# A hybrid decoder step: the attention heads' norm inside the GLU stage, operands split in parts, router products moved, scratch memory shared

## The reference

```python
a = a * lax.rsqrt(jnp.mean(a * a, axis=-1, keepdims=True) + RMS_EPS) * lp['subln_g'] * (1.0 - lam_init)
out = g * jax.nn.sigmoid(g @ w_glu.astype(f32) + b_glu.astype(f32))
mix = jnp.concatenate([a, s], axis=-1) @ lp['w_out']
x = layer_norm(DN_ALPHA * x + mix, lp['ln1_g'], lp['ln1_b'])
```

## Time and profile before

| | us |
|---|---|
| median of 3 runs | 1306.68 (1303.94 to 1307.88) |
| the profiled execution's own time | 1303.61 |
| its span, first to last instruction | 1301.5 |
| head_norm starts (DVE) | 500.07 |
| first GLU product on PE | 518.48 |
| first projection matmul | 556.12 |
| first and last full router transposes | 581.11 and 697.48 |
| ACT's first instruction of `route` | 710.65 |

### The profile page before, as it was taken

How to read it: one execution, slowest core, us unless ns; L and a number is a source line. 1 busy time by engine, 2 the same in 40 slices (tenths; PEclk the granted TensorE clock), 3 DMA queues, 4 the chain that set the end, 5 groups by cost and what they waited for, 6 DMA issues and landing times. The chain is left out here.

```text
span 1301.5 us, 17352 instructions
## 1 busy us (share of the span) xinstructions
PE 1094.6 (84%) x5512; PEld 895.8 (69%) x5513; DVE 689.7 (53%) x1287; ACT 515.4 (40%) x752; POOL 325.7 (25%) x541
## 2 busy tenths in 40 slices
PE   7998999995998695989996258999999999999720
PEld 5886788993666584577774247888888888778510
DVE  3653735503888112445443835544447678675527
ACT  4232321424777312521111043544446567465313
POOL 0807184402000100000000011334233543445315
PEclk9998999996999866988897578999999999999965
DMA  6132221117600402632221074666778799987434
GB/s 223 41 105 53 91 53 50 33 23 278 192 1 1 151 1 72 216 152 97 97 89 54 0 290 157 228 207 206 236 237 309 252 310 411 351 274 245 109 127 164
DMA packets 51249, 201.33 MB, mean 155 GB/s; under 512 B 9107, under 2 KB 15635, under 8 KB 45043
## 3 DMA queue, kind: packets, MB, share of 16 engines
q1 hardware_dynamic: 40674, 138.43, 30.0%
q0 software_dynamic: 7488, 27.27, 8.6%
q10 hardware_dynamic: 3024, 34.87, 6.9%
HBM read 163.81 MB, written 36.73 MB: 154 GB/s over the span
## 5 line engine op out<-in xcount | busy, mean ns | idle before, releaser
L2014 DVE TENSOR_TENSOR wlo<-raw,whi 128x4096 fp32r<-128x4096 f32 x48 | 211.5, 4423 | 95.7 <-ACT whi L1943 95.6
L1943 ACT ACTIVATE whi<-raw 128x4096 fp32r<-128x4096 f32 x48 | 174.9, 3649 | 93.2 <-SPq L1816 38.7
L1852 POOL DMA_INDIRECT acc<-eyb,idxs x25 | 68.1, 2722 | 156.8 <-ACT eyb L1961 156.8
L1885 PE MATMUL psY<-whi,ehs 128*128 128x512 f32 x200 | 82.1, 411 | 9.7 <-DVE wlo L2014 9.7
L1885 PE MATMUL psG<-whi,exs 128*128 128x512 f32 x200 | 83.3, 416 | 4.5 <-DVE exs L2019 4.4
L1887 PE MATMUL psG<-whi,exs 128*128 128x512 f32 x200 | 80.8, 404 | 0.0
L1886 PE MATMUL psG<-wlo,exs 128*128 128x512 f32 x200 | 80.8, 404 | 0.0
L1886 PE MATMUL psY<-wlo,ehs 128*128 128x512 f32 x200 | 79.9, 400 | 0.0
L1887 PE MATMUL psY<-whi,ehs 128*128 128x512 f32 x200 | 79.8, 399 | 0.0
L1885 PE MATMUL psU<-whi,exs 128*128 128x512 f32 x200 | 79.3, 396 | 0.0
L1886 PE MATMUL psU<-wlo,exs 128*128 128x512 f32 x200 | 79.2, 396 | 0.0
(11 more groups left out here) (389 smaller groups left out, 2481.8 us busy)
## 6 DMA issues: line engine op xcount, KB each, us to landing
raw<-in_moe_w_gate SPq DMA_DIRECT2D x16, 2048.0 KB, 8.8
raw<-in_moe_w_up SPq DMA_DIRECT2D x16, 2048.0 KB, 16.7
raw<-in_moe_w_down ACTq DMA_DIRECT2D x16, 2048.0 KB
w_raw<-in_w_in SPq DMA_DIRECT2D x27, 256.0 KB, 3.2
stg<-in_x_prompt SPq DMA_DIRECT2D x8, 512.0 KB, 4.3
kc<-in_cache_k SPq DMA_DIRECT2D x16, 256.0 KB, 3.0
vc<-in_cache_v SPq DMA_DIRECT2D x16, 256.0 KB, 3.0
raw<-in_x_prompt SPq DMA_DIRECT2D x8, 512.0 KB, 6.4
```

The lines of the kernel that those rows point to most:

```text
L1852: nc.gpsimd.indirect_dma_start(s.acc, bass.IndirectOffsetOnAxis(ap=idxs[:, 0:1], axis=0), yb[j][:, :], None, compute_op=ALU.add).then_inc( ...
L1885: pe.matmul(out, hi, w_hi, start=(k == 0), stop=False)
L1943: nc.scalar.activation(whi[:, at], s.raw[:, at], ACT.Copy).then_inc(hi_made[i], 1)
L2014: nc.vector.tensor_tensor(wlo[:, at], s.raw[:, at], whi[:, at].bitcast(F32), ALU.subtract) \
```

## The change

- `head_norm` is removed as a stage; its work moves into `mix`. The scaling of block i + 1 stands on DVE behind the gate product of step i (`scale_o`), the transposes of block i on PE behind GLU product i (`turn_o`), into banks 4 and 5, and the copies on ACT behind tanh i (`keep_o`).
- `wg` is loaded at the end of SP's work in `sample`.
- `high_a` and `low_a` work on parts: part 0 is the four column blocks from `aT`, parts 1 to 4 one column block from `sT` each. For blocks 0 and 1 part 0 is made in step 4, parts 1 to 3 in steps 5, 8 and 11, part 4 at the end. PE waits for each part where it first uses it.
- The projection is issued in halves; the router products of block b - 1 stand between the halves of block b + 1, and `xT` has memory of its own. ACT copies the logits of block b - 1 after the square root and the roundings of block b.
- SP issues `gcol`, the bias, the `w_out` row blocks, and only then the x blocks, the router and LayerNorm weights, the padding rows; expert 0's gate weights wait until all of `o` is scaled, its up weights for the last transposes of `an`, the last GLU product and the padding stores.
- `raw` is allocated before attention and holds `o`, `v`, `wg`, `an`, the zero rows and part of attention's scratch; `kT` and `sT` share `s.ks`.

```diff
 # sample, SP
                 load_pages(sp, io, s, "cache_v", vc, m["v_in"])
+                sp.dma_start(s.wg, io["ssm_w_glu"][0].rearrange("(k p) n -> p k n", p=P)).then_inc(m["glu_in"], 16)
+                sp.wait_ge(m["glu_in"], 16)
 # mix, SP
-                sp.dma_start(wg[:, :, :], io["ssm_w_glu"][0].rearrange("(k p) n -> p k n", p=P)).then_inc(wg_in, 16)
+                sp.dma_start(gcol[:, :], io["subln_g"].rearrange("o v -> v o")).then_inc(g_in, 16)
...
+                sp.wait_ge(scaled, NBLK)
+                sp.dma_start(s.raw[:, slice(*PIECES[0])], expert_weights(io, 0, 0)).then_inc(first_in, 16)
+                sp.wait_ge(o_turned, NBLK)
+                sp.wait_ge(z_made, len(glu))
+                sp.wait_ge(pad_sent, 32)
+                sp.dma_start(s.raw[:, slice(*PIECES[1])], expert_weights(io, 0, 1)).then_inc(first_in, 16)
 # mix, PE
+                def turn_o(b):
+                    r = rows(b)
+                    pe.wait_ge(scaled, b + 1)
+                    if b >= 2:
+                        pe.wait_ge(o_kept, b - 1)
+                    for h in range(H):
+                        last = pe.transpose(bk[4 + b % 2][:, h * P:h * P + r], an[b % 2][0:r, h * P:(h + 1) * P],
+                                            s.ident[0:r, 0:r])
+                    last.then_inc(o_turned, 1)
                     last.then_inc(z_made, 1)
-                pe.wait_ge(s_made, len(glu))
+                    if i < NBLK:
+                        turn_o(i)
...
+                    for k in range(KD):
+                        if half == 0 and (k == 0 or k >= 4):
+                            pe.wait_ge(a_split, part_no(b, max(0, k - 3)) + 1)
...
-                project_out(0)
+                project_half(0, 0)
+                project_half(0, 1)
                 for b in range(NBLK):
                     if b + 1 < NBLK:
-                        project_out(b + 1)
-                    logits(b)
+                        project_half(b + 1, 0)
+                    if b >= 1:
+                        logits(b - 1)
+                    if b + 1 < NBLK:
+                        project_half(b + 1, 1)
+                    turn(b)
+                logits(NBLK - 1)
 # mix, DVE
+                ch(nc.vector.reciprocal(rs[:, :], rs[:, :]))
+                scale_o(0)
                 for i, (k, n) in enumerate(glu):
...
+                    if i + 1 < NBLK:
+                        scale_o(i + 1)
                     if i < KD:
                         dve.wait_ge(w_high, i + 1)
...
+                    if i == 4:
+                        low_a(0, 0)
+                        low_a(1, 0)
+                    if i in (5, 8, 11):
+                        low_a(0, i // 3)
+                        low_a(1, i // 3)
+                low_a(0, parts - 1)
+                low_a(1, parts - 1)
 # mix, ACT
+                    if i < NBLK:
+                        if i == 0:
+                            act.wait_ge(seq, 3)
+                        keep_o(i)
...
                 for b in range(NBLK):
                     r = rows(b)
                     act.wait_ge(var_ready, b + 1)
                     nc.scalar.activation(mv[0:r, 2:3], mv[0:r, 2:3], ACT.Sqrt).then_inc(rooted, 1)
                     if b + 2 < NBLK:
-                        high_a(b + 2)
+                        for p in range(parts):
+                            high_a(b + 2, p)
+                    if b >= 1:
+                        keep_logits(b - 1)
                     act.wait_ge(turned, b + 1)
 # program
+                s.ks = sm("ks", [P, H, L * NC])
+                s.kT = s.ks[:, :, 0:N]
...
                 s.raw = w.enter_context(nc.sbuf_tensor("raw", [P, WCOLS], F32, side="right"))
+                s.o = s.raw[:, 0:V_AT].rearrange("p (b c) -> p b c", b=NBLK)
+                s.v = s.raw[:, V_AT:2 * V_AT].rearrange("p (b c) -> p b c", b=NBLK)
+                s.wg = s.raw[:, WG_AT:WG_AT + W // P * W].rearrange("p (k n) -> p k n", k=W // P)
+                attention(nc, io, s)
                 mix(nc, io, s)
```

More of the change, by code:

```diff
@@ L91, in attend @@
         Ex = [[sb(f"Ex{k}{j}", [P, SEQ]) for j in range(2)] for k in range(2)]
-        w = [sb(f"w{k}", [P, SEQ]) for k in range(2)]
-        wT = [sb(f"wT{k}", [P, SEQ]) for k in range(2)]
+        w = [s.raw[:, SHARE_AT + k * SEQ:SHARE_AT + (k + 1) * SEQ] for k in range(2)]
+        wT = [s.raw[:, SHARE_AT + 2 * SEQ:SHARE_AT + 3 * SEQ], sb("wT1", [P, SEQ])]
         mx = sb("mx", [P, len(steps), 2])
@@ L298, in sample @@
         sg = sb("sg", [P, 1])
-        qf = sb("qf", [P, H, P])
+        qf = s.raw[:, V_AT:V_AT + H * P].rearrange("p (h c) -> p h c", h=H)
         qm = sb("qm", [P, H, NB_DEC, P])
-        Ex = [sb(f"sE{k}", [P, KC]) for k in range(2)]
-        PT = [sb(f"sPT{k}", [P, 3 * NS]) for k in range(2)]
+        share = s.raw[:, SHARE_AT + NB_DEC * NPG * P:]
+        Ex = [share[:, KC * k:KC * (k + 1)] for k in range(2)]
+        PT = [share[:, 2 * KC + 3 * NS * k:2 * KC + 3 * NS * (k + 1)] for k in range(2)]
         oT = [sb(f"soT{k}", [P, NS]) for k in range(2)]
@@ L1310, in mix @@
     glu = [(k, n) for k in range(W // P) for n in range(3)]
+    parts = 1 + W // P
     with ExitStack() as c:
@@ L1327, in mix @@
         tg = [sb(f"tg{k}", [P, 512]) for k in range(2)]
[L1328 removed]
         rr = [sb(f"mr{k}", [P, D]) for k in range(2)]
[L1331 removed]
+        xT = [sb(f"mxT{k}", [P, KD, P]) for k in range(2)]
+        wg = s.wg
+        an = [s.raw[:, V_AT + k * W:V_AT + (k + 1) * W] for k in range(2)]
+        nul = s.raw[:, DOWN_AT - 512:DOWN_AT]
         lg, lb, xn0, xn1 = (s.raw[:, DOWN_AT + k * D:DOWN_AT + (k + 1) * D] for k in range(4))
@@ L1345, in mix, with part_no @@
         x_out = [sem(f"mi_xo{k}") for k in range(2)]
+        def part_no(b, p):
+            return 2 * p + b if b < 2 else parts * b + p
         with nc.Block() as block:
@@ L1360, in _ @@
                 sp.dma_start(lb[:, :], io["ln1_b"].to_broadcast([P, D])).then_inc(l_in, 16)
-                for i in range(2):
-                    sp.dma_start(s.raw[:, slice(*PIECES[i])], expert_weights(io, 0, i)).then_inc(first_in, 16)
                 sp.wait_ge(nul_set, 1)
@@ L1421, in logits @@
                     last.then_inc(turned, 1)
+                def logits(b):
+                    r = rows(b)
                     pe.wait_ge(t_kept, b + 1)
@@ L1443, in _, with scale_o, low_a @@
             def _(dve):
+                ch = Chain(dve, seq)
+                def scale_o(b):
+                    r = rows(b)
+                    if b >= 2:
+                        dve.wait_ge(o_turned, b - 1)
+                    for h in range(H):
+                        last = nc.vector.tensor_scalar(an[b % 2][0:r, h * P:(h + 1) * P], s.o[0:r, b, h * P:(h + 1) * P],
+                                                       rs[0:r, b * H + h:b * H + h + 1], None, ALU.mult)
+                    last.then_inc(scaled, 1)
+                def low_a(b, p):
+                    r = rows(b)
+                    dve.wait_ge(a_high, part_no(b, p) + 1)
+                    hi, lo = ap[b % 2]
+                    if p == 0:
+                        last = nc.vector.tensor_tensor(lo[:, 0:4, 0:r], s.aT[:, :, b * P:b * P + r],
+                                                       hi[:, 0:4, 0:r].bitcast(F32), ALU.subtract)
+                    else:
+                        dst, high = (part[:, 3 + p, 0:r].rearrange("p (n t) -> p n t", t=L) for part in (lo, hi))
+                        last = nc.vector.scalar_tensor_tensor(dst, s_block(b)[:, p - 1, :, :], 0.25, high.bitcast(F32),
+                                                              ALU.mult, ALU.subtract)
+                    last.then_inc(a_split, 1)
+                ch(nc.vector.memset(s.ss[NS:P, QB, :], 1.0))
+                nc.vector.tensor_scalar(rs[:, :], s.ss[:, :, :].rearrange("p b h -> p (b h)"), 1.0 / P, EPS,
+                                        ALU.mult, ALU.add).then_inc(ss_ready, 1)
+                dve.wait_ge(g_in, 16)
+                ch(nc.vector.tensor_scalar(gcol[:, :], gcol[:, :], 1.0 - LAM_INIT, None, ALU.mult))
+                dve.wait_ge(ss_rooted, 1)
+                ch(nc.vector.reciprocal(rs[:, :], rs[:, :]))
+                scale_o(0)
                 for i, (k, n) in enumerate(glu):
@@ L1527, in _ @@
                     if b + 2 < NBLK:
-                        high_a(b + 2)
+                        for p in range(parts):
+                            high_a(b + 2, p)
+                    if b >= 1:
+                        keep_logits(b - 1)
                     act.wait_ge(turned, b + 1)
-                    if b >= 2:
-                        act.wait_ge(l_made, b - 1)
                     for half in range(2):
```

189 lines of the change are left out of this document (69 added, 120 removed).

## The result

The changed kernel takes **1257.91 us** (median of 4 runs, 1252.94 to 1262.81) against 1305.31 (4 runs, 1300.55 to 1307.88) for the kernel before on the same chip: ratio **0.9638**, 95% interval 0.9597 to 0.9679, so some 47 us less.

What follows compares the result with a forecast made beforehand. PE's chain through barrier-separated stages was taken to bound the kernel: -11.7 - 4.4 - 2.2 - 12.6 - 1.0 = -31.9 us, 1271.7 from the profiled 1303.61; plus 3.1 for the median gives 1274.8 us, range 1266 to 1288.

Steps and rivals of the forecast that it cites:

- norm and GLU to the last product: Head norm inside the GLU stage, weights loaded early: last GLU product ends at 539.3 against 551.03, -11.7 us.
- wait before the projection: Before the projection, operands split in parts: PE waits 0.7 us in place of 5.12, -4.4 us.
- half-clock start of the projection: First 13 projection matmuls: half-clock start gone as PE hardly pauses, -2.2 us, bounds 0 and -2.2.
- seven cycles: Projection and router cycles, router products moved: 1.17 us wait gone from each, three clock falls left, 103.8 against 116.37, -12.6 us.
- last block's root: Stage's end: DVE's 1.33 us wait for the last block's square root falls to some 0.3, -1.0 us.
- So from 0 to 7 falls; I take 3: Projection and router cycles: three of seven still have a clock fall, each costing 1.53 us.
- mirror case: Projection and router cycles: no clock fall at all, total -36.5 us, 1270 us; chance 0.13.
- Eight take 1.44 us at the full clock, so 0.72 a block: GLU stage: price of the head norm's transposes on PE, about 6.1 us for nine groups of four.
- 0.6 of stall: GLU stage, fifth step: PE stalls 0.6 us as rounding and low part of the attention columns come in.
- second rival: GLU stage: w_out's transfers through two buffers set the pace, costing 12 us, 1287 us; chance 0.14.
- Third rival: Projection loop: long half-clock stretches from two interruptions a cycle; with all matmuls it costs 57 us, 1327 us; chance 0.03.
- Part 5: Memory layout, with scratch, v, o and GLU weights in the raw buffer: taken as 0, bound 1 us either way.

Runs made afterwards that it cites:

- parts_late: Changed kernel with operand parts of blocks 0 and 1 made only after the last gate product, one wait for PE: 1259.51 us, ratio 0.9658.
- wg_late: Changed kernel with the GLU weights loaded as first transfer of the GLU stage instead of in the sampling stage: 1267.85 us, ratio 0.9704.
- norm_apart: Changed kernel with the head norm a stage of its own again, expert 0's gate weights not waiting for the scaling: 1269.35 us, ratio 0.9714.
- consts_early: Changed kernel with the routing stage's five tables loaded one stage earlier: 1254.83 us, ratio 0.9623.
- only_moved: Kernel before with only the router products, and ACT's copy of them, moved between halves of the next projection but one: 1287.48 us, ratio 0.9849.
- adjacent: Changed kernel with router products of block b - 1 directly behind the transposes of block b: 1262.22 us, ratio 0.9661.
- logits_behind: Changed kernel with router products put back directly behind the same block's transposes: 1280.27 us, ratio 0.9822.
- logits_twice: Changed kernel with the eight router matmuls of each block done twice: 1287.56 us, ratio 0.9850.
- memory_only: Kernel before with only the change's memory layout, xT's own memory, SP's order in the GLU stage and expert 0's late weights: 1304.04 us, ratio 1.0001.

## Why the prediction was too high, point by point

| term | predicted | measured (first profiles) |
|---|---|---|
| norm and GLU to the last product | -11.7 | 37.25 for 51.03: -13.8 |
| wait before the projection | -4.4 | 0.66 for 5.12: -4.4 |
| half-clock start of the projection | -2.2 | 22.50 for 24.99: -2.5 |
| seven cycles | -12.6 | 97.03 for 116.37: -19.3 |
| last block's root | -1.0 | 12.18 for 13.17: -1.0 |
| sum | -31.9 | -41.0 |
| ahead of these stages | 0 | -3.7 (5 profiles each) |
| behind them | 0 | +0.2 (5 profiles each) |

Every mechanism named went the way it was named. Two terms were mis-sized, 9.1 us together, and 7.8 us lay outside the sum: the forecast was 1274.8, the time 1257.9, 16.9 less.

**Seven cycles, 6.7 of the 9.1 us missed.** The failing step is "So from 0 to 7 falls; I take 3". There were none: the cycles took 13.7 to 13.9 us in all five profiles of after, and in `parts_late`, `wg_late`, `norm_apart`, `consts_early`, `only_moved` and `adjacent`. Of the two rows it was built on, the experts' stage, where the clock stays at 1.00 among transposes, was the one that applied, and the fall after a pause of 1.49 us wasn't, for the wait was exactly what went. 3 x 1.53 = 4.6 us hang on this. The other 2.0 are the cycle's length: 13.88 and not 14.17 = 15.34 - 1.17. Subtracting the wait left in what the wait also costs on its edges: PE-busy time of a cycle without a fall is 14.13 with the wait (`logits_behind`) and 13.88 without, because records overlap where nothing stands between them. The mirror case (no fall, -36.5, 1270) was thus the right one and was given 0.13; with its other terms as they were it is still 12 us above the time.

**Norm and GLU, 2.1 of it.** The step is "Eight take 1.44 us at the full clock, so 0.72 a block". That row holds waits that it doesn't print: the profile merged two blocks and the short idle time between them. PEld (PE's weight loads) shows them in the kernel before, for the same eight transposes and the start of the next ones:

```profile
508.07 0.42 PEld L554 LDWEIGHTS psA<-identz,an 128*128 128x128 f32 x4 [0.73 <-DVE an L542]
508.85 0.42 PEld L554 LDWEIGHTS psA<-identz,an 128*128 128x128 f32 x4 [0.36 <-DVE an L542]
509.69 0.42 PEld L554 LDWEIGHTS psA<-identz,an 128*128 128x128 f32 x4 [0.42 <-DVE an L542]
```

A block is 0.42 us of loads and then a wait for DVE's scaling, which takes 0.83 a block and sets the pace of 0.78 to 0.84. In the changed kernel, where the scaled block is mostly there, four transposes cost 0.44 between matmuls, up to 0.50 behind the waits and in the eighth group, and the smaller last ones 0.39: 4.1 us for the nine groups and not 6.1. The 0.6 of stall assumed came as 0.8, in two places, and the products took 32.3 us for 32.55. The ring of w_out held with the margin the count gave: ACT waited for it twice, 0.41 us at 512.48 and 0.16 at 527.29, and PE for neither. The second rival, ring-paced, is refuted. The drain that the Trainium skill (ScalarE: Activation LUTs, What ACT_TABLE_LOAD costs) adds to a table change isn't in this trace either: tanh 0.02 us behind the load, at 505.80.

**Projection's wait and start: right,** and by the mechanism given. `parts_late` shows the two tied together: with a wait of 3.86 us, a clock fall comes back with it and costs 1.5 us.

**Third rival (slower by long half-clock stretches):** refuted, with a clock of 1.00 over 97 us. The nearest to it are longer falls in single cycles: 18.80 us for 15.67 in `logits_twice`, and the first cycle of `memory_only`, with the old order, 18.45 us for 15.32.

**Part 5 and the rest of the program.** Memory at 0 was right for its direct effect, and "Later stages should keep their lengths" held (590.6 and 590.8). Had each term been sized right, the forecast would have been 1306.7 - 41.0 = 1265.7, still 7.8 above the measured 1257.9. Of these, 1.4 is the median of before itself (1305.3 in this comparison), 3.7 the shorter stretch ahead of the changed stages, for which the sum had no term and whose cause is open, and 2.7 is in no profile: it is about what separates the profiled executions of after (1260.5) from the median.

**Do the parts add up?** Undone one at a time they cost 20.1 + 4.2 + 5.75 + 5.35 = 35.4 of 41.2. The difference is what a single undoing leaves in place: the GLU products at the full clock in `norm_apart` (2.8), and in `parts_late` the 2.7 worked out there. With these it is 40.9. Both are differences between single profiles, so this is a check on the size and no proof of each part.

## What to carry to other kernels

Where an engine waits briefly in each turn of a loop, look at the granted clock of the turn with and without a fall before pricing the wait: here 1.17 us of waiting, seven times 1.17 = 8.2 us, was worth 19.3 when it went, and giving PE the result of the previous turn to work on removed it. Small products need not be kept away from transposes, but several groups of them in a row, or behind a wait, should be broken up by full-width matmuls. Price small work that goes between matmuls from the distance of starts where nothing waits: a printed group can hold short waits for another engine, as the 1.44 us did.

## What the runs showed of the hardware

- The clock can fall with PE busy all the time (`logits_twice`). With 32 products of 16 columns in a row, 3.64 us at the full clock, it fell in six of seven cycles (0.90, one of 0.82), at about 1.55 us each, 3.13 for the long one; with 16 of them, 1.85 us, the transposes in front or not, in none.
- Transposes of 128x128 in float32 cost about 0.1 us each at the full clock: four between matmuls 0.44 us, eight in a row 0.81. At the full clock a 512-column projection matmul costs 0.23, at half 0.43.
- Transposes alone brought the clock up: in `norm_apart` PE did nothing but the norm's 36 transposes, and the granted clock was 0.50 in the first eight and 1.00 from 511.06 on.
- Prompt attention, with the same instructions in every kernel here, took 112 or 115 us at a granted clock of 0.97 or 0.94, the kernel before both from one execution to the next. The long ones had two or three clock falls more. That alone is 3 us of scatter.
